# Dense products of a split-precision kernel: five matmuls a weight tile instead of six, with the low half added at evacuation

## The reference

```python
# D_MODEL 1024, D_FF 2816, D_GMLP 2048, 16 heads
for i in range(2):
    x = x + 0.5 * swiglu(rms_norm(x, g[i,0]), w_gate[i,0], w_up[i,0], w_down[i,0])
    h = rms_norm(x, g[i,1])
    x = x + (gmlp_mixer(h) if i == 0 else latent_attention(h))
    x = x + 0.5 * swiglu(rms_norm(x, g[i,2]), w_gate[i,1], w_up[i,1], w_down[i,1])
# swiglu(h) = (silu(h @ w_gate) * (h @ w_up)) @ w_down
# gmlp: u, v = gelu(h @ w_in + b); v = rms_norm(v); (u * spatial_mix(v)) @ w_out
```

## Time and profile before

| | |
|---|---|
| median of 3 runs | 2402.55 us (2399.73 to 2407.85) |
| profiled execution, first to last instruction | 2398.6 us |
| PE busy | 2338.9 us (98%), 18230 matmul records |
| DVE, ACT, POOL busy | 910.6, 691.8, 415.4 us |
| mean granted TensorE clock | 0.995 of full |
| dense matmuls of L539 in the chain that ended last | 77% |

### The profile page before, as it was taken

How to read it: one execution, slowest core, us unless ns; L and a number is a source line. 1 busy time by engine, 2 the same in 40 slices (tenths; PEclk the granted TensorE clock), 3 DMA queues, 4 the chain that set the end, 5 groups by cost and what they waited for, 6 DMA issues and landing times.

```text
span 2398.6 us, 42939 instructions
## 1 busy us (share of the span) xinstructions
PE 2338.9 (98%) x18230; PEld 2206.1 (92%) x18230; DVE 910.6 (38%) x1054; ACT 691.8 (29%) x851; POOL 415.4 (17%) x352
## 2 busy tenths in 40 slices
PE   7999999999999999999999999999999999999998
PEld 6999999999999999999999999986548469999998
DVE  5333334344443333334333335534354444333332
ACT  4212224432233222134212124432232233212122
POOL 3202112222222112022202012210010012202010
PEclk9999999999999999999999999999999999999999
DMA  4232223222222222323222324221102012222321
GB/s 148 92 101 88 88 83 94 88 88 87 74 89 88 88 88 93 101 70 106 88 88 94 99 79 122 63 59 39 36 18 71 1 36 88 88 88 91 103 79 63
DMA packets 197944, 194.53 MB, mean 81 GB/s; under 512 B 11656, under 2 KB 195637, under 8 KB 197573
## 3 DMA queue, kind: packets, MB, share of 16 engines
q1 hardware_dynamic: 194138, 191.38, 25.4%
q10 hardware_dynamic: 3434, 1.42, 0.3%
q0 software_dynamic: 256, 0.07, 0.0%
HBM read 190.23 MB, written 2.63 MB: 80 GB/s over the span
## 4 chain that ended last, share of the span: by engine, by line
PE 93%; DVE 3%; ACT 1%; POOL 1%; issue 1%; DMA 0%; SPq 0%; ACTq 0%; POOLq 0%; DVEq 0%
PE main L539 77%; PE main L879 2%; PE main L878 2%; PE side L943 1%; PE main L742 1%; PE side L919 1%; PE side L726 1%; PE main L796 1%; PE side L951 1%; PE side L899 1%; PE main L850 1%; PE side L669 1%; PE main L787 1%; PE side L774 1%; POOL square_sum L1674 0%
## 5 line engine op out<-in xcount | busy, mean ns | idle before, releaser
L539 PE MATMUL main<-xg_hi,w_hi 128*128 128x260 f32 x3392 | 686.3, 283 | 7.2 <-DVE w_lo L1329 6.4
L539 PE MATMUL main<-xg_hi,w_lo 128*128 128x260 f32 x3392 | 684.4, 283 | 0.0
L539 PE MATMUL main<-xg_lo,w_hi 128*128 128x260 f32 x3392 | 683.2, 283 | 0.0
L539 PEld LDWEIGHTS main<-xg_hi,w_hi 128*128 128x128 f32 x3392 | 524.2, 189 | 8.1 <-DVE w_lo L1329 6.5
L539 PEld LDWEIGHTS main<-xg_hi,w_lo 128*128 128x128 f32 x3392 | 523.8, 189 | 0.0
L1249 DVE TENSOR_TENSOR w_lo<-raw,w_hi 128x2048 fp32r<-128x2048 f32 x167 | 383.8, 2298 | 365.5 <-ACT w_hi L987 359.5
L539 PEld LDWEIGHTS main<-xg_lo,w_hi 128*128 128x128 f32 x3392 | 522.4, 189 | 0.0
L987 ACT ACTIVATE w_hi<-raw 128x2048 fp32r<-128x2048 f32 x163 | 310.5, 1905 | 345.2 <-PE main L539 345.2
L539 PE MATMUL main<-h_hi,w_hi 128*128 128x260 f32 x1920 | 386.9, 283 | 2.8 <-POOL h_lo L1681 2.8
L539 PE MATMUL main<-h_hi,w_lo 128*128 128x260 f32 x1920 | 386.9, 283 | 0.0
L539 PE MATMUL main<-h_lo,w_hi 128*128 128x260 f32 x1920 | 385.7, 282 | 0.0
(11 more groups left out here) (256 smaller groups left out, 1517.5 us busy)
## 6 DMA issues: line engine op xcount, KB each, us to landing
raw<-in_ffn_w_gate SPq DMA_DIRECT2D x44, 1024.0 KB, 5.3
raw<-in_ffn_w_up SPq DMA_DIRECT2D x44, 1024.0 KB, 5.3
raw<-in_ffn_w_down SPq DMA_DIRECT2D x32, 1024.0 KB, 5.1
raw<-in_gmlp_w_in SPq DMA_DIRECT2D x16, 1024.0 KB, 5.4
raw<-in_ffn_w_down SPq DMA_DIRECT2D x16, 768.0 KB, 4.4
raw<-in_gmlp_w_out SPq DMA_DIRECT2D x8, 1024.0 KB, 5.3
raw<-in_mla_w_o SPq DMA_DIRECT2D x8, 1024.0 KB, 5.6
over<-in_cache_mla SPq DMA_DIRECT2D x64, 104.0 KB, 1.9
```

The costliest lines, as they stand in the source:

```text
L539: mm = nc.tensor.matmul(main[:, m, half, 0:HALF], w[:, k, m * P:(m + 1) * P], moving[:, k, half * HALF:(half + 1) * HALF], start=(k == 0 a ...
```

## The change

Both halves of an activation block lie side by side (`xg`, `hs`), so that the high and the low half form one run of 1040 columns. The new `wide_tile` streams these against `w_hi` in three matmuls (348, 344 and 348 columns), and the high half against `w_lo` in two (260 and 260). The outcome is two sums of 520 columns in three banks of PSUM a tile, `high` and `low`; the middle matmul writes the end of one and the start of the other in the shared bank. Two tiles take six banks; `side` keeps two of its own (6 and 7) and shares two. At evacuation the two sums are added: gate, up and v tiles by an ACT copy of `low` into a single buffer `low_in`, a DVE addition of `high`, and the former DVE multiplication, now from SBUF; down tiles by two DVE additions to `x` instead of one. All `ffn` tiles, the gMLP's v tiles and its output product use it: 4 x 528 + 128 + 128 = 2368 of the 2656 steps. Where a stage that had used the banks otherwise comes before, and at the first tile of each `ffn`, PE waits for the last tile's evacuation too (`fresh`).

```diff
+CUT = 348
+REST = TOK - CUT
+ENTRY = 512 - CUT
...
-        h_hi = sb("h_hi", [P, KC, TOK], F32R, operands)
-        h_lo = sb("h_lo", [P, KC, TOK], F32R, operands)
+        hs = sb("hs", [P, KC, 2, TOK], F32R, operands)
+        h_hi, h_lo = hs[:, :, 0, :], hs[:, :, 1, :]
...
+        xg = sb("xg", [P, KD, 2, TOK], F32R, early)
+        xg_hi, xg_lo = xg[:, :, 0, :], xg[:, :, 1, :]
...
+        banks = ctx.enter_context(nc.psum_tensor("banks", [P, 8, 512], F32))
+        main = banks[:, 0:4, :].rearrange("p (m a) n -> p m a n", m=2)
+        side = banks[:, 4:8, :]
+        high, low = (banks[:, 0:6, :].rearrange("p (m b) n -> p m (b n)", m=2)[:, :, c0:c0 + TOK]
+                     for c0 in (ENTRY, 2 * 512 - REST))
+        seam = banks[:, 0:6, :].rearrange("p (m b) n -> p m (b n)", m=2)[:, :, 512:512 + 2 * (512 - REST)]            .rearrange("p m (a n) -> p m a n", a=2)
...
+            def wide_tile(m, slot, k_tiles, moving, before=None, free=None):
+                if free is not None:
+                    pe.wait_ge(evac_done, free)
+                ws = [w[:, slot, :].rearrange("p (k c) -> p k c", k=KC)[:, :, m * P:(m + 1) * P] for w in (w_hi, w_lo)]
+                both = moving[:, :, :, :].rearrange("p k a n -> p k (a n)")
+                for k in range(k_tiles):
+                    if before and k in before:
+                        before[k]()
+                    first, last = k == 0, k == k_tiles - 1
+                    nc.tensor.matmul(high[:, m, 0:CUT], ws[0][:, k, :], both[:, k, 0:CUT], start=first, stop=False)
+                    nc.tensor.matmul(seam[:, m, :, 0:REST], ws[0][:, k, :], both[:, k, CUT:TOK + REST], start=first, stop=last)
+                    nc.tensor.matmul(low[:, m, REST:TOK], ws[0][:, k, :], both[:, k, TOK + REST:2 * TOK], start=first, stop=False)
+                    nc.tensor.matmul(high[:, m, 0:HALF], ws[1][:, k, :], both[:, k, 0:HALF], start=False, stop=last)
+                    mm = nc.tensor.matmul(low[:, m, HALF:TOK], ws[1][:, k, :], both[:, k, HALF:TOK], start=False, stop=last)
+                mm.then_inc(tile_done, 1)
...
+                    if whole:
+                        wide_tile(m, slot, k_tiles, hs, before=before, free=e + m - 1 + (fresh and m == 0))
+                    else:
+                        out_tile(m, slot, k_tiles, h_hi, h_lo, before=before, free=e + m - 1)
...
-                                out_tile(m, s, KD, xg_hi, xg_lo, before=before, free=e + 4 * i + 2 * s + m - 1)
+                                fresh = rms_at and s == 0 and m == 0
+                                wide_tile(m, s, KD, xg, before=before, free=e + 4 * i + 2 * s + m - (0 if fresh else 1))
...
-                    out_tile(m, s, KD, xg_hi, xg_lo, before=before, free=e + 4 * i + 2 * s + m - 1)
+                    wide_tile(m, s, KD, xg, before=before, free=e + 4 * i + 2 * s + m - 1)
...
+            pe.wait_ge(root_done, at_gmlp.rms + 1)
...
-                            down(n, e, at_gmlp.h, KC, slot=s)
+                            down(n, e, at_gmlp.h, KC, slot=s, whole=True, fresh=i == 0 and s == 0)
...
-                pe.wait_ge(evac_done, at_end.evac - KD + k + 1)
+                pe.wait_ge(evac_done, at_end.evac - 1 if k == 0 else at_end.evac - KD + k + 1)
...
+            def take_low(m, t, w):
+                act.wait_ge(tile_done, t)
+                act.wait_ge(high_used, w)
+                nc.scalar.activation(low_in[:], low[:, m, :], ACT.Copy).then_inc(low_set, 1)
...
                         for m in range(2):
+                            take_low(m, t + 4 * i + m + 1, w + 4 * i + m)
                             act.wait_ge(evac_done, e + 4 * i + m + 1)
                             nc.scalar.activation(tmp_act[:, m, :], tmp_in[:, m, :], ACT.Silu).then_inc(act_done, 1)
...
+            def whole_tile(dst, m, count, w):
+                dve.wait_ge(low_set, count)
+                nc.vector.tensor_tensor(dst, high[:, m, :], low_in[:], ALU.add).then_inc(high_used, 1)
+                dve.wait_ge(high_used, w)
+            def scaled_whole(m, count, w):
+                whole_tile(tmp_in[:, m, :], m, count, w)
+                nc.vector.tensor_tensor(tmp_in[:, m, :], tmp_in[:, m, :], rstd_all[:], ALU.mult).then_inc(evac_done, 1)
...
+                if w is not None:
+                    dve.wait_ge(tile_done, t)
+                    xk = x[:, bass.ds(k, 1), :].rearrange("p a n -> p (a n)")
+                    nc.vector.scalar_tensor_tensor(xk, high[:, m, :], scale, xk, ALU.mult, ALU.add).then_inc(high_used, 1)
+                    dve.wait_ge(high_used, w)
+                    nc.vector.scalar_tensor_tensor(xk, low[:, m, :], scale, xk, ALU.mult, ALU.add).then_inc(evac_done, 1)
+                    return
...
+                            scaled_whole(m, lows + 4 * i + m + 1, w + 4 * i + m + 1)
                         split_ahead(n, i, 1)
                         for m in range(2):
-                            dve.wait_ge(tile_done, t + 4 * i + m + 3)
-                            dve.wait_ge(mul_done, h + 2 * i + m + 1)
-                            nc.vector.tensor_tensor(halves(tmp_h[:, m, :]), main[:, m, :, 0:HALF],
-                                                    halves(tmp_mul[:, m, :]), ALU.mult).then_inc(evac_done, 1)
+                            dve.wait_ge(mul_done, h0 + 2 * i + m + 1)
+                            whole_tile(tmp_h[:, m, :], m, lows + 4 * i + m + 3, w + 4 * i + m + 3)
+                            nc.vector.tensor_tensor(tmp_h[:, m, :], tmp_h[:, m, :], tmp_mul[:, m, :],
+                                                    ALU.mult).then_inc(evac_done, 1)
```

More of the change, by code:

```diff
@@ L95, in ffn_past @@
     chunks = 2 * pairs + 4 * len(FF_GROUPS)
-    return at.past(chunks, 2 * chunks, 2 * chunks, 2 * pairs, 2 * pairs, 2 * pairs, 1, 1, 0 if last else KD)
+    return at.past(chunks, 2 * chunks, 2 * chunks, 2 * pairs, 2 * pairs, 2 * pairs, 1, 1, 0 if last else KD, 2 * chunks, 4 * pairs)
 def bc(ap, n):
@@ L260, in program @@
         evac_done = sem("evac_done")
+        low_set = sem("low_set")
+        high_used = sem("high_used")
         act_done = sem("act_done")
@@ L548, in go @@
                     for half in range(2):
-                        mm = nc.tensor.matmul(side[:, half, 0:HALF], ones, square_sum[:, half * HALF:(half + 1) * HALF],
+                        mm = nc.tensor.matmul(side[:, bank + half, 0:HALF], ones, square_sum[:, half * HALF:(half + 1) * HALF],
                                               start=True, stop=True)
@@ L552, in rms, with down @@
                 return go
-            def down(n, e, h, k_tiles, m_tiles=2, slot=0):
+            def down(n, e, h0, k_tiles, slot=0, whole=False, fresh=False):
                 pe.wait_ge(lo_done, n + 1)
@@ L651, in _ @@
                 pe.wait_ge(vg_done, 2 * g + 2)
+                if g == NG // 2:
+                    pe.wait_ge(evac_done, e)
                 if g == 0:
@@ L673, in _ @@
             for i in range(4):
-                down(n, e, at_gmlp.h + KC, KC, slot=i % 2)
+                down(n, e, at_gmlp.h + KC, KC, slot=i % 2, whole=True, fresh=i == 0)
                 n, e = n + 1, e + 2
@@ L683, in _ @@
             out_tile(0, 0, KD, xg_hi, xg_lo, free=e - 1,
-                     before={4: rms(at_mla), KD - 2: lambda: pe.wait_ge(xg_lo_done, KD * at_mla.norm + KD)})
+                     before={4: rms(at_mla, 0), KD - 2: lambda: pe.wait_ge(xg_lo_done, KD * at_mla.norm + KD)})
             out_tile(1, 0, KD, xg_hi, xg_lo, free=e)
@@ L1016, in ffn, with gate_up @@
             def ffn(at, after, final=False):
-                n, t, e, h, a = at.chunk, at.tile, at.evac, at.h, at.act
+                n, t, e, h, a, w = at.chunk, at.tile, at.evac, at.h, at.act, at.whole
                 for g, pairs in enumerate(FF_GROUPS):
-                    def gate_up(i, first=False, n=n, t=t, e=e, h=h):
+                    def gate_up(i, first=False, n=n, t=t, e=e, w=w):
                         split_ahead(n, i, 0, t)
@@ L1066, in v_chunk @@
                     j = 4 * i + 2 * s + m
+                    take_low(m, t + j + 1, at_gmlp.whole + j)
                     act.wait_ge(evac_done, e + j + 1)
@@ L1288, in down_loop, with gate_up @@
                         for m in range(2):
-                            add_to_x(4 * i + 2 * s + m, m, t + 4 * i + 2 * s + m + 1, scale)
+                            add_to_x(4 * i + 2 * s + m, m, t + 4 * i + 2 * s + m + 1, scale,
+                                     None if w is None else w + 4 * i + 2 * s + m + 1)
             def ffn(at, after, final=False):
-                n, t, h = at.chunk, at.tile, at.mul
+                n, t, h0, w, lows = at.chunk, at.tile, at.mul, at.whole, at.low
                 for g, pairs in enumerate(FF_GROUPS):
-                    def gate_up(i, first=False, n=n, t=t, h=h):
+                    def gate_up(i, first=False, n=n, h0=h0, w=w, lows=lows):
                         split_ahead(n, i, 0)
@@ L1332, in _ @@
```

(4 more changed lines are left out.)

78 lines of the change are left out of this document (38 added, 40 removed).

## The result

The changed kernel takes **2421.01 us** in the median of 5 runs (2411.76 to 2423.22), the kernel before 2400.61 (2399.73 to 2407.85) beside it: ratio **1.0063**, 95% interval [1.0038, 1.0088]. In a second comparison (experiment 4, 9 runs against 26) it was 2420.9 us, 1.0046 [1.0026, 1.0067]. I had forecast 2408, with an own range of 2399 to 2416 that the result missed, and in all a range of 2376 to 2434, wide enough to hold two of the rivals. The profiled execution spans 2418.8 us.

The account below looks back on a forecast made before the run. PE, busy 98% with dense matmuls, was taken as the bound. Savings of 26 us against added waits and clock loss summed to +5.0: span 2403.6, plus 4.0 to the median, 2408 us; own range 2399 to 2416, in all 2376 to 2434.

Parts of the forecast that it names:

- no gain: Rival for the dense matmuls: the rest goes with columns, or the new form costs the saving; 2433 us, chance 0.17.
- The 4.0 us I had added from span to median: Final addition: the median of the runs lies 4.0 us above the profiled span, taking 2403.6 to 2408.
- The dense step: Dense matmuls on PE: one instruction less saves 11 ns a step, over 2368 steps -26 us (24 to 28).
- The line through 260 and 512: Matmul times of 120.1 and 227 ns at these column counts, giving 157.4 ns for 348 columns and 155.7 for 344.
- The norm loop: 6-block down chunks ahead of a norm: DVE and ACT turn goes from 8.20 to 9.66 us and leads; +18 us.
- Waits for `h_lo`: From last up tile to `h_lo`: way 3.32 to 4.73 us; +4.6 in 8-block chunks, +1.45 for the last `ffn`.
- Row sum of v: The gMLP's v row sum waits behind one more copy and multiplication, less cover: +1.4 us.
- after the gMLP's output product: 8-block chunks where PE still leads; only the last tile's longer read-out shows, +0.9 us.
- The clock: Three long norm waits each bring half clock for 3.4 us, 1.5 us lost each: +4.5 us (0 to 5).
- The load rules: Rival: 120 ns is the weight load, which longer matmuls hide; step 673.5 ns, 2329 us, faster, chance 0.10.
- Half the waits: Rival: loop turn ahead of norms shorter than 9.66 us, clock kept, waits cost half; 2391 us, chance 0.13.

Follow-up runs that it names:

- experiment 4: The changed kernel run once more, unchanged, for comparison on the same chip: 2420.9 us, 1.0046 of the kernel before.
- experiment 3: The changed kernel with `CUT` 264 in place of 348, so matmuls of 264, 512, 264, 260 and 260 columns: 2426.35 us, 1.0079 of the kernel before.
- experiment 5: As experiment 3, with the 512-column matmul given as two of 256 in every block but a tile's first: 2442.52 us, 1.0148 of the kernel before.
- Experiments 1: The changed kernel with an odd down tile's norm work held back until after the next chunk's weight split: 2405.14 us, 1.0004 of the kernel before.
- experiment 2: The kernel before, six matmuls, with a second dependent addition to x (factor 0.0) per down tile ahead of a norm: 2416.2 us, 1.0053.
- experiment 7: The kernel before with only the norm order changed, an odd tile's norm work held back: 2406.43 us, 0.9992 of the kernel before.
- experiment 8: The changed kernel with `hs` moved by 64 bytes, the weights and `xg` behind it by 128: 2422.98 us, 1.0065 of the kernel before.

## Why the prediction was right, and which of its terms was not

The sign and the place were right. The time was 13 us above my number: outside my own range of 2399 to 2416, and inside the stated one only because that reached up to the "no gain" rival. The most likely outcome I had named, no change within 0.3% (0.43), didn't come; slower (0.39) did. Of the 15.2 us between the profiled span (2418.8) and my 2403.6, 9.7 are the attention stage, and in the traces without attention I was 5.5 us short. The 4.0 us I had added from span to median were 2.2.

- **The dense step, mis-sized.** "I take 11 ns", from a rest taken as nearly constant at 128, 260 and 512 columns. A step went from 720.2 to 711.8 ns, **8.4 ns**, so -19.9 us and not -26. These 6 us are as much as the whole shortfall; the other errors, below, nearly cancel (some 2 us more of clock, 2 less of waits for `h_lo`, 0.9 less at the start). The rest isn't constant: it is 11 to 17 ns at 264 to 348 columns and 19 at 512 (experiment 3), and an instruction by itself is worth 5 to 6 ns (experiment 5). The line through 260 and 512 failed at its upper end: I read about 227 ns off one pair of 16-row matmuls, and 512 columns in this stream take 232.4. With that value the same line gives 159.2 ns at 348, a step of 716, 4 ns too long the other way: the matmuls of 344 and 260 columns took 154.7, 119.1 and 118.0 ns, less than the line has. So my 11 ns came as near as they did by two errors against one another.
- **The norm loop: right.** Turn 9.67 us against 9.66, PE idle at its three ends 2.4 to 3.8 us. The `ffn` stages give it: ffn0 is 2.1 us longer, and 5.4 (the loop, as forecast) + 0.7 (two 8-block waits) - 4.0 (476 steps of 8.4 ns, those in the loop saving nothing) is 2.1. Experiments 1 and 2 show it from both sides.
- **Waits for `h_lo`: right in kind.** 8-block chunks 0.26 to 0.41 us idle where I had 0.47 and 0.1 for weights, in all 2.6 us and not 4.6; 6-block chunks 1.73 where I had 1.89. ffn3, which has no norm behind it, came out 1.9 us shorter; -4.4 + 1.45 + 0.7 is -2.2.
- **Row sum of v, and after the gMLP's output product: right.** 2.08 us idle against 0.71 is +1.4 as said; 1.62 against 0.62 is +1.0, I had 0.9.
- **The clock: size right, cause not shown.** I had three dips of 1.5 us. Between start and tail there are four outside the attention stage, the fourth at 515.9 us after the 2.08 us wait for v's squares. Each costs 1.5 to 1.7 us by the stages. My way to 1.5 was off: half a clock loses less than half the time, since 260 columns take 216.8 ns there (experiment 7, 11 matmuls) against 120.0, which makes 1.5 us in 3.4. That a long wait brings the dip on, and that one of up to 1 us doesn't, is not borne out: experiment 2 had three waits of 2.4 us and one dip, experiment 7 a dip behind 0.71 us.
- **What I didn't see:** that the attention stage by itself takes 10 us more or less from one execution to the next. The pair of profiled executions overstates the change by that much (the runs of experiment 4 differ by 11.6 us in their fastest and 12.5 in their means); a difference of spans is no measurement of an edit in this kernel.
- **Rivals.** The load rules: fell, 711.8 and not 675. No gain: fell as well, 8.4 of 11 ns arrive, though the time itself lies as near to its 2433 as to my 2408. Half the waits: fell by the turn of 9.67.

## What to carry to other kernels

When an edit buys TensorE time with work on another engine, read that engine's turn in the stage where it is nearest to the bound, and write down the dependent chain through it: 0.7 us a tile on an engine 38% busy cost 12 us. What was lost in this way can mostly be had back by order (hold half of the follow-up work by a tile, run early blocks of both tiles ahead of a wait); try that before giving up the edit. And a price per instruction is measured by splitting one instruction and keeping the columns, in the stream itself. Where two traces are compared, the stretches at half clock of each have to be counted first.

## What was unexpected of the hardware

- Matmuls of the same form differ by block, by up to 8 ns (3rd of a step: 154.2 to 162.5; 5th: 115.0 to 120.0), exactly repeating with period 4, where blocks lie 4160 bytes apart; moving `hs` by 64 bytes and the weights by 128 shifts the pattern on `hs` (experiment 8).
- The granted clock in a stage with the same code was half for 20 us in one execution and for 44 us in others (experiment 7 against before), about 10 us of time.
- At the 1.2 GHz level the rest beyond the columns is gone: 260 columns take 216.8 ns from start to start (experiment 7), which is 260 columns at 1.2 GHz, and 344 take 286.7 (after, 3 matmuls).
